# Table of expert weights in DRAM laid out by blocks of 64 tokens

## The reference

```python
q = (xb @ w_pq).reshape(PEER_BLOCK, PEER_HEADS, 2, PEER_DKH)
s = jnp.einsum('thpd,hpkd->thpk', q, sub_keys).astype(jnp.float32)
sv, si = lax.top_k(s, PEER_TOPK)
...
cidx = (si[:, :, 0, :, None] * N_KEYS + si[:, :, 1, None, :]).reshape(PEER_BLOCK, PEER_HEADS, -1)
best, pos = lax.top_k(cand, PEER_TOPK)
eidx = jnp.take_along_axis(cidx, pos, axis=-1)
g = jax.nn.softmax(best, axis=-1)
act = jax.nn.gelu(jnp.einsum('thkd,td->thk', expert_u[eidx], xb).astype(jnp.float32), approximate=False)
return jnp.einsum('thk,thkd->td', (g * act).astype(xb.dtype), expert_v[eidx])
```

## Time and profile before

| | |
|---|---|
| profiled execution, device time | 4299.12 us |
| its span | 4297.5 us |
| mean granted TensorE clock | 0.935 |
| TensorE busy | 3665.7 us (85%) |
| VectorE busy | 2620.5 us (61%) |
| ScalarE busy | 1562.8 us (36%) |
| spread_stage, first to last table copy | 3138.3 to 3334.3 us |
| experts_stage, first issue to end of span | 3355.2 to 4297.5 us |

### The profile page before, as it was taken

The page is one execution under the profiler, slowest core; times in us unless marked ns, Lnnn a source line. Parts: engine busy times, 40 slices in busy tenths (PEclk is TensorE's granted clock), DMA queues, the critical chain, the costliest instruction groups (busy, mean ns, idle before and its releaser), DMA issues. The chain is left out here.

```text
span 4297.5 us, 50663 instructions
## 1 busy us (share of the span) xinstructions
PE 3665.7 (85%) x17647; PEld 3051.1 (71%) x17647; DVE 2620.5 (61%) x5041; ACT 1562.8 (36%) x2763; POOL 562.1 (13%) x513
## 2 busy tenths in 40 slices
PE   1988899699958888987897987968877799999998
PEld 0656777588746667775786755657867688888887
DVE  4676424377545653246775645539977477777777
ACT  2344434232234443423232333422266233333332
POOL 0000000101000000001001110034300122223333
PEclk8999999899979999998998988989888899999999
DMA  4422122245211111214452200022245788888887
GB/s 182 146 89 67 45 74 84 95 164 215 88 60 59 31 52 60 73 49 185 157 190 72 66 16 6 16 78 95 90 141 158 268 299 303 317 308 303 292 320 262
DMA packets 270170, 598.72 MB, mean 139 GB/s; under 512 B 117248, under 2 KB 145664, under 8 KB 267392
## 3 DMA queue, kind: packets, MB, share of 16 engines
q1 hardware_dynamic: 214080, 392.47, 26.3%
q0 software_dynamic: 55872, 203.45, 13.3%
HBM read 559.15 MB, written 36.70 MB: 139 GB/s over the span
## 5 line engine op out<-in xcount | busy, mean ns | idle before, releaser
L324 PE MATMUL ps<-mix_w,mix_h 128*128 128x384 f32 (+1 forms) x2304 | 539.7, 384 | 94.7 <-DVE mix_w L737 75.4
L324 PEld LDWEIGHTS ps<-mix_w,mix_h 128*128 128x128 f32 x2304 | 425.9, 197 | 201.8 <-DVE mix_w L737 82.8
L3052 PE MATMUL ps<-peer_v,peer_coef 128*128 128x512 f32 x2304 | 542.0, 391 | 9.8 <-DVE peer_coef L3167 9.8
L3052 PEld LDWEIGHTS ps<-peer_v,peer_coef 128*128 128x128 f32 x2304 | 432.2, 188 | 97.0 <-issue 10.1
L1113 PE MATMUL ps<-mix_h,mlp_u 128*128 128x512 f32 x1536 | 360.5, 396 | 87.5 <-DVEq L1209 87.4
L3041 PE MATMUL ps<-peer_h,peer_u 128*128 128x384 f32 x2208 | 401.0, 336 | 20.6 <-PEq L102 20.6
L3041 PEld LDWEIGHTS ps<-peer_h,peer_u 128*128 128x128 f32 x2208 | 388.9, 188 | 27.8 <-issue 20.9
L1113 PEld LDWEIGHTS ps<-mix_h,mlp_u 128*128 128x128 f32 x1536 | 292.9, 191 | 154.0 <-DVEq L1209 92.7
L1124 PE MATMUL ps<-mlp_coef,mlp_v 128*128 128x512 f32 x1536 | 355.2, 392 | 19.5 <-DVEq L1220 19.5
L1124 PEld LDWEIGHTS ps<-mlp_coef,mlp_v 128*128 128x128 f32 x1536 | 291.3, 190 | 81.2 <-DVEq L1220 20.3
L737 DVE TENSOR_TENSOR mix_w<-mix_raw,mix_w 128x1024 fp32r<-128x1024 f32 (+1 forms) x164 | 185.1, 1145 | 265.9 <-ACT mix_w L537 265.6
(11 more groups left out here) (526 smaller groups left out, 6275.2 us busy)
## 6 DMA issues: line engine op xcount, KB each, us to landing
peer_raw_v<-in_v_tiles SPq DMA_DIRECT2D x128, 512.0 KB
peer_raw_u<-in_u_tiles SPq DMA_DIRECT2D x104, 512.0 KB, 4.8
mlp_tiles<-in_w_ada POOLq DMA_DIRECT2D x96, 512.0 KB, 4.6
mix_raw<-in_w_rest SPq DMA_DIRECT2D x68, 512.0 KB, 3.5
mlp_raw_u<-in_w_up SPq DMA_DIRECT2D x64, 512.0 KB, 9.1
mlp_raw_v<-in_w_down SPq DMA_DIRECT2D x16, 2048.0 KB, 7.9
mix_raw<-in_w_a SPq DMA_DIRECT2D x48, 512.0 KB, 4.2
expert_weights<-peer_table SPq DMA_DIRECT2D x6, 4096.0 KB, 20.9
```

The lines of the kernel that those rows point to most:

```text
L324: last = pe.matmul(proj(u, n_cols), M.H[:, x, k, b * P:(b + 1) * P], V.w[:, y, i % SLOTS_W, k % 2 * n_cols:(k % 2 + 1) * n_cols], start=k ...
L3052: last = pe.matmul(bank(M.ps, 2 * b + half), Q.coef[:, x, t % 4, b * P:(b + 1) * P], Q.v[:, y, t % 4, half * BANK:(half + 1) * BANK], star ...
```

## The change

The table in DRAM gets another layout. Before it is [j, i, token], with 384 tokens to a row: a store of one side writes, for each i and j, a run of 64 tokens (256 bytes), and a weight load of four j reads for each i and j a run of 384 tokens (1536 bytes). After it is [side number 0 to 5, i, j, 64 tokens]: a store writes one block of 4 MB, for each i one run of 32 KB, as `Q.table` has it, and a weight load reads, for each i and each of six blocks, four j of 64 tokens, a run of 1 KB. `Q.weight` has the new order too, and `scale` addresses the 384 tokens as 6 x 64. Size of every transfer, number of DMAs, order of the streams and all waits stay.

```diff
-    Q.coef, Q.weight = at("coef", 150, 2, 4, DENSE, dt=F32R), at("weight", 162, 8, DENSE)
+    Q.coef, Q.weight = at("coef", 150, 2, 4, DENSE, dt=F32R), at("weight", 162, 2, DENSE * 2 // P, 4, P // 2)
...
                     sp.wait_ge(laid, 2 * (g + 1))
-                    b, side = divmod(n, 2)
-                    sp.dma_start(spread_dram.rearrange("j i t -> i j t")[:, :, b * P + side * HALF_T:
-                                                                         b * P + (side + 1) * HALF_T],
-                                 Q.table[:, side, :, :]).then_inc(M.kept[side], 16)
+                    sp.dma_start(spread_dram[n], Q.table[:, n % 2, :, :]).then_inc(M.kept[n % 2], 16)
...
-                sp.dma_start(Q.weight[:, g % 2 * G:g % 2 * G + G],
-                             spread_dram[g * G:(g + 1) * G].rearrange("j i t -> i j t")).then_inc(w_here[g % 2], 16)
+                sp.dma_start(Q.weight[:, g % 2], spread_dram[:, :, g * G:(g + 1) * G].rearrange("s i j t -> i s j t")).then_inc(
+                    w_here[g % 2], 16)
...
-                dve.tensor_tensor(Q.act[:, t % 4], Q.act[:, t % 4], Q.weight[:, g % 2 * G + t % G],
-                                  ALU.mult).then_inc(scaled, 1)
+                opened = Q.act[:, t % 4].rearrange("p (s t) -> p s t", t=P // 2)
+                dve.tensor_tensor(opened, opened, Q.weight[:, g % 2, :, t % G], ALU.mult).then_inc(scaled, 1)
...
-    spread_dram = nc.dram_tensor("expert_weights", (NKEYS, P, DENSE), F32, kind="Internal").ap()
+    spread_dram = nc.dram_tensor("expert_weights", (DENSE * 2 // P, P, NKEYS, P // 2), F32, kind="Internal").ap()
```

## The result

The changed kernel takes 4248.22 us (median of 4 runs, 4240.37 to 4251.60) against 4299.61 us: ratio 0.9877, 95% interval 0.9863 to 0.9891, faster by 51.4 us or 1.2%. The forecast was 4239, the range 4228 to 4264. The profiled execution of after took 4247.12 us, its span is 4245.4.

The account below looks back on a forecast made before the run. The bound was taken to be the table store, 16,384 runs of 256 bytes, holding up SyncE's queue. Savings of 49.8 + 10.8 = 60.6 us gave 4299.6 - 60.6 = 4239 us, range 4228 to 4264.

Parts of the forecast that it names:

- Part 1: Six table stores in spread_stage: 32 KB runs cut the data time from 19.2 to 10.2 us, saving 49.8 us.
- S: Issue time of a table store on SyncE's queue; the next `raw_u` tile was forecast at S + 13.7, wanted at S + 13.9.
- rival A: Table stores reach only about 300 GB/s, five stops of 3.6 us stay: 4260; chance with similar cases 0.10.
- B: Writes to the table stay at 218 GB/s whatever the runs: 4291; chance with other small gains 0.08.
- count of bus cycles: Skill's count for table stores: 11 cycles per 256 byte packet, 3 overhead, so large packets at most 11/8 as fast.
- Part 2: Boundary from spread_stage to experts_stage: last `keep` no longer blocks, 7.0 MB at 395 GB/s decide; 10.8 us saved.
- Part 4: The 128 `scale` multiplies in experts_stage: reading weights as 6 x 64 costs 0 to +30 ns each, taken as nothing.
- Part 3: The 32 weight loads: +0.2 us each, hidden inside experts_stage; two uncovered at the boundary cost 0.4 us.
- the cover: Slack of weight loads in experts_stage: wanted four tiles later, engines 85% busy, so each may grow by 4.2 us.
- rival C: Power of two spacing slows weight loads until experts_stage is DMA-bound: 4413 at 65 GB/s; chance 0.05.
- The rule on row pitch: Skill's rule on large power of two pitches: about 2 us more per weight load, 4 at the boundary, sum 4243.
- the line of the prediction: DMA packet time fitted through 256 byte and 4 KB packets: 9.7 ns + 0.0354 ns per byte.

Follow-up runs that it names:

- e9_store_twice: Changed kernel with each table store doubled, the same 4 MB going first to a second DRAM tensor through the same queue; 4309.07 us (one run).
- e8_pool_store: Kernel before with its 256 byte runs, but table stores issued by GpSimd in four pieces of 1 MB each, through another queue; 4281.34 us.
- e6_store_256: Changed kernel with the old stores (256 byte runs) and the new weight loads (1 KB runs); 4317.74 us against 4298.82 for the kernel before.
- e1_pad: Changed kernel with 4 KB of padding behind each 32 KB run of the table in DRAM; 4242.16 us.
- e10_block_pad: Changed kernel with 4 KB of padding behind each 4 MB block of the table and none inside it; 4244.37 us.
- e2_load_1536: Changed kernel with the new stores but the old form of the weight loads (512 runs of 1536 bytes); 4239.71 us.
- e0_after_again: Changed kernel unaltered, measured again; 4251.18 us, single runs 4245.79 to 4263.56.
- e3_act_first: Changed kernel with eight loads of kept activations issued ahead of the weight load instead of behind it; 4233.90 us.
- e5_groups: Changed kernel with another table layout: stores in 4096 runs of 1 KB, weight loads in 128 runs of 6 KB; 4253.76 us.

## Why the prediction was right, and where it was not

**The bound** was named rightly: the stores' time in the queue ahead of a `raw_u` tile. e9_store_twice (stops without a blocked issue) and e8_pool_store (small packets in another queue, no stops) show it from both sides.

**Part 1** forecast 49.8 us, 48.5 were measured (171.8 to 123.3). The rate of 32 KB runs was 406 GB/s; a store landed in 12.1 us, forecast 11.9. The tile came at S + 14.7 instead of 13.7, so of the stop of 10 us there remains 0.8, with 3.0 us in three waits over all five sides, where 0.2 each were forecast. VectorE was busy for 23.8 us per side instead of 24.2 and idle for 0.9, so two small misses partly cancel in the 24.7 us of a side (forecast 24.4). The prediction took its rate from stores "without a short run"; in fact 48 of those 425 packets are under 512 bytes. Rivals A and B fell with the 406 GB/s. So did the Trainium skill's count of bus cycles (DMA: Bandwidth & Descriptors, "Why small descriptors are slow (HBM only)"): large packets are 1.86 times as fast here (406 / 218), not 11/8 times.

**Part 2** forecast 10.8 us, measured 45.0 - 34.3 = 10.7, though the rate there was 372 GB/s, not 395. SyncE left spread_stage 5.1 us after the store, not 3.5, and the DMA engines were full all the same (share 1.00 from 3290 to 3314): the bytes decided. 7.0 MB at 372 GB/s would take 18.8 us, one more than the sum has, so the agreement to 0.1 us is in part luck.

**Part 4** was right: `scale` takes 551 ns as before.

**Part 3 is the step that failed.** It said that the loads are covered as long as one grows by less than 4.2 us, and put their cost inside experts_stage at nothing; measured were 8.7 us (926.9 - 918.2), 6.2 of them idle TensorE, and 3.1 more in the busy time of downs (545.1 us against 542.0), of which the slow matmuls at 3979.77 alone are 1.7. The growth itself was undersized: but for the addressing of `scale`, before and e6_store_256 differ only in the loads, and there the median landing goes from 5.5 us to 7.7, by 2.2 us, where +0.2 was taken and +1.6 was the upper bound; 1.3 or more of it go with the spacing (7.7 to 6.4 in e1_pad). But 2.2 is still under the 4.2 that the prediction called covered, and the stage lost time all the same: what was wrong is the cover.

The prediction measured the cover by how long the weights themselves can wait and by how full the engines are on average. Neither limits here; the limit is the small load behind the weight load in the same queue, with 3.4 us from issue to use, and it had none to spare: the row of `scale` in the earlier trace rows shows 9.3 us of waiting for `early_acts` already in the kernel before. The prediction used that row for its 551 ns and left its last column unread. Of rival C the direction was right, the spacing costs something, but not its mechanism: the stage is not DMA-bound (share 0.83 from 3850 to 4000 us), and the loads landed in 7.7 us in the median (e6_store_256), not in over 10. But a mean share hides that the DMA engines are nearly full just while the small load waits behind the weight load (0.93 from 3734.3 to 3742.8).

**The rule on row pitch** (Trainium skill, DMA: Bandwidth & Descriptors, "Latency and other measured facts"), which the prediction weighed as 2 us per load: e1_pad bears it out in kind, in that 4 KB of padding per row undoes the loss. But the page's rows are of pitches of 512 KiB and more from partition to partition, with padding tried at 4 MiB; here partitions lie 32 KB apart, and padding the 4 MB blocks alone (e10_block_pad) undid only part of the loss. The 2 us per load are near the 2.2 us of landing measured; the 4 us at the boundary did not show (34.3 us with padding and without, 34.0 with the old loads in e2_load_1536).

The total came 9 us above the forecast in the medians, 4248.2 against 4239. In the profiled executions it is 8.5 us: 8.7 from part 3, 1.3 from part 1, 0.1 from part 2, less 1.7 by the part ahead of the first store, which is scatter. The total lies inside the range, but part 3's 8.7 us were allowed for by no term of it; the range held them only because it was wide enough above for rival A, and that is luck: the execution of e0_after_again that lost 17.4 us took 4263.56, with the range ending at 4264.

## What to carry to other kernels

When a transfer gets slower, or longer, look at what is issued behind it in the same queue and how soon that is wanted, not only at when the transfer itself is wanted; a wait that costs nothing yet (9.3 us in one row) says where the cover is already used up. A small transfer that is wanted at once (here 192 KB against 768) belongs ahead of the bulk one; here that order (e3_act_first), worth nothing before the change, is worth 14 to 17 us in the medians after it. And a layout that turns short runs into long ones on one side can make them shorter or wider apart on the other: where the new spacing is a power of two, padding is worth a try.

## What was not expected of the hardware

Stores from SBUF to DRAM lie near one line in the size of their packets: 18.8 ns for 256 bytes, 46.9 for 1 KB (e5_groups), 155 for 4 KB, 16 x 32,768 / 406 = 1291 ns for 32 KB, where the line of the prediction says 1170. A weight load in 1 KB runs with 32 KB from partition to partition lands 1.3 us later than with 36 KB (7.7 in e6_store_256 with the old stores, 6.4 in e1_pad with the new). A queue that holds a store of 256 packets per engine delays the next issue too, by 7 us (e5_groups), while behind one of 8 per engine the next issue took 0.32 us. And an issue queue need not be blocked for a tile to be late: in e9_store_twice the issues behind the stores took 1.24 us or less, and ScalarE waited 53.8 us.
